# Layer 0 and layer 1 attention scores: distance bias added by VectorE instead of by flip products, with B's scores in two PSUM banks

## Chip, core and metric
The kernel runs on one core of a Trainium2 chip. Its time is the device time of one execution in microseconds (us), lower is better. The engines are TensorE (PE: matrix products and transposes; PEld is its weight load), VectorE (DVE), ScalarE (ACT), GpSimd (POOL) and SyncE (SP), whose queue issues nearly all DMAs. Each engine takes its own instructions in order, and semaphores join them.

## What is computed
A decoder trunk of two layers on 512 tokens of width 1024. Layer 0 has A (attention with a forget gate, 8 heads) and B (sliding window of 128, sinks, distance bias, 8 heads), layer 1 has C (sparse attention with a top-k mask and a distance bias, 8 heads) and D (latent attention, 8 heads). After each pair comes an output projection, then an MLP of width 4096. The change concerns the logits of B and C:

```python
# B: bias by distance, one sink logit per head in the softmax
bias = bias_table[_t5_bucket(jnp.maximum(dist, 0))]
logits = jnp.where(mask[None, :, None, None], logits + bias, -jnp.inf)
p = jax.nn.softmax(jnp.concatenate([logits, sink], axis=-1), axis=-1)[..., :-1]
# C: keys picked by top-k, bias by distance
bias = bias_table[_t5_bucket(jnp.maximum(dist, 0))].transpose(0, 1, 3, 2).astype(jnp.float32)
logits = jnp.where((dist >= 0)[:, :, None, :], logits + bias, -jnp.inf)
p = jax.nn.softmax(logits, axis=-1)
```

## The kernel before
Activations lie transposed in SBUF. Every fp32 operand is split into a rounded high part and a low remainder, and a product is three fp32r products (`product`, L677 to L679: high by high, low by high, high by low). A weight slab is 128 columns of a weight matrix: SP loads it (`load_slab`), ACT makes the high part (`split_slab`, L1161), POOL the low part (L1604), PE takes 8 tiles of it (24 products of 512 columns).

The heads are numbered j: A is 0 to 7, B 8 to 15, D 16 to 23, C 24 to 31. Both attention phases are software pipelines written out by hand, one step s per head. In step s of layer 0 (`first_step`), PE does scores(s+2), then the input slabs of that step (`SLABS_AT`: 18 in step 9, none in step 8 or from 10 on), then tiles of the output projection where `OUT_TILES_AT` places them as filling (steps 10 to 15), then values(s), then the transposes of the probabilities of head s+1 (`turn_probs`, L863). ACT does output_half(s-1), the high part of the transposed probabilities of s (`probs_hi`), the exponentials of s+2 (L1348) and output_hi(s-1). DVE does outputs_summed(s-1) (L2020), the low parts (`probs_lo`, L1795), then for B the reciprocal and the scaling of head s+1 (`normalise`, L1997 and L2004) and last the maxima of s+2 (L1986). In layer 1 (`heads`) the order is the same with fewer parts: DVE does probs_lo(s), maxima(s+2), outputs_summed(s-1), sums(s+2). The scaling goes through a diagonal that POOL makes, and PE's turning of the probabilities is L861.

Scores land in PSUM banks 0, 1 and 2 (`units(j)` says which query block stands where). scores(j) may write bank b once the exponentials of head j-1 have read it (L779, `exp_done`). The bias of a head comes from a row of 1024 words in DRAM (`bias_rows`), of which partition p reads a piece that starts at word p. That gives the strip in reversed query order. ACT makes its high part (`strip`, L1161), POOL its low part (`prepare`), and PE multiplies both with a reversed identity, `flip_r`, which turns the order round and adds the bias into the score bank: L789, L790, L792 to L795 for B, L816 and L817 for C. B's sink is a column beside each unit's scores, so its units are 130 or 258 columns wide.

Behind the heads of layer 0, slabs 19 and 20 are finished with the last tile of the attention output, slab 21 has its own spare place (`W_SPARE`), and slab 22 needs slot 0, which slab 20 holds. ACT splits slab 22 in `out_projection` only after the square and the rounding of output tile 0.

## Time and profile before
| | us |
|---|---|
| median of 3 runs (1240.57 to 1241.54) | 1240.57 |
| the profiled execution's own time | 1240.66 |
| its span, first to last instruction | 1238.9 |
| mean granted TensorE clock | 0.988 of full speed |

The profile is a page (busy time, chain, costliest groups) and a trace that answers questions. A timeline row has the start and the length of an instruction or of a run of equal ones (xN), its engine, line, operation, output<-inputs with sizes, and in square brackets how long its engine had been idle and who released it. Lengths of products overlap, since they are pipelined. What one costs a busy PE is the distance between two starts. PEclk is the share of the full 2.4 GHz granted in a window, and 0.5 is its other level, 1.2 GHz.

### The profile page before, as it was taken

Reading aid. Unit: us, or ns where it says so; the run is one execution under the profiler, and the core shown is the slowest. Engines: PE = TensorE matmul, PEld = TensorE weight load, DVE = VectorE, ACT = ScalarE, POOL = GpSimd, SP = SyncE. Lnnn points to the kernel's source line nnn. Section 1 sums busy time; section 2 is a strip of 40 time slices with the busy share of each in tenths; the row PEclk is TensorE's granted clock in tenths of the full one; section 3 lists DMA queues with packets and bytes.
Section 4 is the critical chain, followed back from the end, with each engine's and each line's share of the span. In section 5 each row is a group of like instructions: output and inputs, shape, how many; then the busy total and the mean of one; then the engine's idle time right before and its main releaser. Section 6 shows DMA issues by size and latency. Waiting matters only on the chain.

```text
span 1238.9 us, 16061 instructions
## 1 busy us (share of the span) xinstructions
PE 1193.5 (96%) x5744; PEld 983.7 (79%) x5749; DVE 674.3 (54%) x1023; ACT 515.3 (42%) x919; POOL 538.0 (43%) x291
## 2 busy tenths in 40 slices
PE   7999996999999999999998899999999999999997
PEld 5688885878888888888776678888788888888886
DVE  5766675665144154165669889556651441541654
ACT  6677575433222222224363467864332222222233
POOL 2333432334444444447632466434344444444441
PEclk9999998999999999999998999999999999999998
DMA  5222220333333333333312101102233333333332
GB/s 157 71 68 73 65 69 32 97 85 103 100 88 102 102 88 99 102 90 96 87 50 68 52 17 35 36 18 68 85 102 99 89 102 102 89 98 102 92 95 85
DMA packets 188922, 100.83 MB, mean 81 GB/s; under 512 B 8806, under 2 KB 186257, under 8 KB 188866
## 3 DMA queue, kind: packets, MB, share of 16 engines
q1 hardware_dynamic: 187596, 99.97, 28.0%
q8 instruction: 34, 0.56, 0.2%
q10 hardware_dynamic: 1270, 0.13, 0.1%
q14 instruction: 22, 0.18, 0.0%
HBM read 97.92 MB, written 2.16 MB: 81 GB/s over the span
## 4 chain that ended last, share of the span: by engine, by line
PE 74%; DVE 6%; ACT 3%; issue 1%; POOL 1%; DMA 0%; ACTq 0%; DVEq 0%; SPq 0%
PE bank L677 23%; PE bank L678 22%; PE bank L679 22%; PE bank L861 3%; DVE score L2101 1%; DVE best L2097 1%; ACT ur L1161 1%; ACT probs L1348 1%; POOL wl L1604 1%; DVE sqsum L1859 1%; PE bank L822 0%; ACT wh L1161 0%; PE bank L873 0%; PE bank L816 0%; PE bank L874 0%
## 5 line engine op out<-in xcount | busy, mean ns | idle before, releaser
L1604 POOL TENSOR_TENSOR wl<-raw,wh 128x1024 fp32r<-128x1024 f32 x172 | 419.7, 2441 | 554.1 <-ACT wh L1161 554.0
L677 PE MATMUL bank<-ur,wh 128*128 128x512 f32 x1080 | 422.2, 391 | 0.2 <-POOL wl L1604 0.2
L678 PE MATMUL bank<-ur,wh 128*128 128x512 f32 x1080 | 420.7, 390 | 0.0
L679 PE MATMUL bank<-ur,wl 128*128 128x512 f32 x1080 | 420.7, 390 | 0.0
L1161 ACT ACTIVATE wh<-raw 128x1024 fp32r<-128x1024 f32 x172 | 181.7, 1058 | 508.3 <-PE bank L679 508.1
L677 PEld LDWEIGHTS bank<-ur,wh 128*128 128x128 f32 x1080 | 203.2, 188 | 43.2 <-issue 1.1
L678 PEld LDWEIGHTS bank<-ur,wh 128*128 128x128 f32 x1080 | 203.2, 188 | 42.1 <-issue 0.5
L679 PEld LDWEIGHTS bank<-ur,wl 128*128 128x128 f32 x1080 | 203.0, 188 | 42.2
L1959 DVE TENSOR_TENSOR xT<-bank,xT 128x512 f32<-128x512 f32 x64 | 44.3, 692 | 227.6 <-PE bank L679 227.5
L1795 DVE TENSOR_TENSOR ur<-sq,ur 128x512 fp32r<-128x512 f32 x65 | 130.1, 2001 | 45.4 <-ACT ur L1161 45.4
L677 PE MATMUL bank<-xh,wh 128*128 128x512 f32 (+1 forms) x296 | 122.5, 414 | 5.3 <-DVE xl L1865 2.9
L678 PE MATMUL bank<-xl,wh 128*128 128x512 f32 (+1 forms) x296 | 117.3, 396 | 0.0
L679 PE MATMUL bank<-xh,wl 128*128 128x512 f32 (+1 forms) x296 | 117.3, 396 | 0.0
L1950 DVE TENSOR_TENSOR tbuf<-bank,rstd 128x512 f32<-128x512 f32 x64 | 44.2, 691 | 91.8 <-PE bank L679 91.4
L1348 ACT ACTIVATE probs<-bank,negmax 128x256 f32<-128x256 f32 (+5 forms) x128 | 63.5, 507 | 35.9 <-DVE negmax L1986 35.1
L677 PEld LDWEIGHTS bank<-xh,wh 128*128 128x128 f32 (+1 forms) x296 | 56.2, 190 | 23.0 <-issue 10.6
L1161 ACT ACTIVATE ur<-sq 128x512 fp32r<-128x512 f32 (+1 forms) x80 | 50.6, 632 | 39.2 <-DVE sq L1954 38.2
L679 PEld LDWEIGHTS bank<-xh,wl 128*128 128x128 f32 (+1 forms) x296 | 56.2, 190 | 13.1
L678 PEld LDWEIGHTS bank<-xl,wh 128*128 128x128 f32 (+1 forms) x296 | 56.3, 190 | 12.3 <-issue 1.3
L1795 DVE TENSOR_TENSOR probT_l<-bank,probT_h 128x512 fp32r<-128x512 f32 (+1 forms) x88 | 49.1, 600 | 27.6 <-ACT probT_h L1161 27.1
L1859 DVE TENSOR_TENSOR sqsum<-sqsum,sq 128x512 f32<-128x512 f32 x28 | 49.3, 1759 | 19.8 <-ACT sq L1200 19.8
L1986 DVE TENSOR_REDUCE negmax<-bank 128x1 f32<-128x256 f32 (+5 forms) x128 | 51.4, 458 | 6.0 <-PE bank L823 4.9
(226 smaller groups left out, 1365.4 us busy)
## 6 DMA issues: line engine op xcount, KB each, us to landing
raw<-in_w_mlp SPq DMA_DIRECT2D x128, 512.0 KB, 3.8
raw<-in_w_in_e SPq DMA_DIRECT2D x18, 512.0 KB, 3.6
raw<-in_w_in_o SPq DMA_DIRECT2D x10, 512.0 KB, 3.7
raw<-in_w_out_e SPq DMA_DIRECT2D x8, 512.0 KB, 3.7
raw<-in_w_out_o SPq DMA_DIRECT2D x8, 512.0 KB, 3.8
strip_raw<-bias_rows SPq DMA_DIRECT2D x8, 256.0 KB, 3.0
out<-probs SPq DMA_DIRECT2D x4, 512.0 KB, 2.6
probs<-in_x SPq DMA_DIRECT2D x2, 512.0 KB, 4.3
```

The lines of the kernel that those rows point to most:

```text
L677: mm(dst, lhs[0], rhs[0], start=start, stop=False, skip_group_check=not check)
L678: mm(dst, lhs[0], rhs[1], start=False, stop=False, skip_group_check=not check)
L679: return mm(dst, lhs[1], rhs[0], start=False, stop=stop, skip_group_check=not check)
L861: done = mm(dst, probs[:, slot, c:c + P], diag[slot][:, q:q + P], start=True, stop=True)
L1161: return nc.scalar.activation(dst, src, ACT.Copy, scale=scale)
L1348: e = nc.scalar.activation(probs[:, slot, pc:pc + w], bank[b][:, col:col + w], ACT.Exp, bias=negmax[:, slot, blk:blk + 1], accum_out=expsu ...
L1604: return nc.gpsimd.tensor_tensor(dst, a, b, ALU.subtract)
L1795: return v.tensor_tensor(dst, a, f(b), ALU.subtract)
L1859: v.tensor_tensor(sqsum[:, :], sqsum[:, :], sq[:, m % 2, :], ALU.add).then_inc(sq_added, 1)
L1950: v.tensor_tensor(t, ps, rstd[:, :], ALU.mult).then_inc(slab_taken, 1)
L1959: v.tensor_tensor(xT[:, m, :], ps, xT[:, m, :], ALU.add).then_inc(slab_taken, 1)
L1986: m = v.reduce_max(negmax[:, j % 2, blk:blk + 1], bank[b][:, col:col + w], AX.X, negate=True)
```

## The change
Seven edits belong together.

1. The rows of `bias_rows` are copied in DRAM 128 times each (`spread_bias`, 16 DMAs on SP's queue in steps -1 to 10), into `skew_b` and `skew_c`, whose pitch is one word longer than the copy. Reading with a pitch one shorter gives partition p a piece that starts p words earlier, in true order.
2. The flip products go, with `strip` on ACT, the strip part of `prepare` on POOL, and `strip_h` and `strip_l`.
3. DVE's maximum of a unit in B and C becomes one operation that computes -(score + bias), writes it back to the bank, and takes the minimum with a start value (the negated sink for B). The exponential then scales by -1.
4. The sink leaves the columns: ACT makes exp(sink - max) for 4 blocks (`sink_exp`), DVE adds it to the sums.
5. B's scores use banks 0 and 1 only, and slab 21's result goes to bank 2, so its tiles may run among the B heads.
6. The order of DVE in B changes: maxima(s+2) before probs_lo(s), and normalise(s+2) at the end of step s instead of normalise(s+1). Step 8 does both 9 and 10.
7. 14 tiles of the projection stand in steps 10 to 15 instead of 9, and the spare split of slab 21 moves from step 12 to step 10.

```diff
-SPARE_STEP = 12
-OUT_TILES_AT = {10: ((0, 0, 1),), 11: ((0, 1, 2),), 12: ((0, 2, 3),), 13: ((0, 3, 4),), 14: ((0, 4, 6),), 15: ((1, 0, 3),)}
-LAST_OUT_TILES = ((1, 3, 7), (0, 6, 7), (2, 0, 1))
+SPREAD_AT = {s: (2 * s + 2, 2 * s + 3) for s in range(-1, 3)}
+SPREAD_AT.update({s: (s + 5,) for s in range(3, 11)})
+SPARE_STEP = 10
+OUT_TILES_AT = {10: ((0, 0, 2),), 11: ((0, 2, 4),), 12: ((1, 0, 3),), 13: ((1, 3, 4), (2, 0, 1)), 14: ((2, 1, 4),),
+                15: ((0, 4, 6),)}
+LAST_OUT_TILES = ((1, 4, 7), (2, 4, 7), (0, 6, 7))
...
-                return [(0, 0, 0, 130, 0), (1, 0, 130, 258, 130), (2, 1, 0, 258, 388), (3, 2, 0, 258, 646)]
+                return [(0, 0, 0, 128, 0), (1, 0, 128, 256, 128), (2, 1, 0, 256, 384), (3, 1, 256, 256, 640)]
...
+            def spread_bias(i):
+                h = i % NH
+                rows, off, width = (skew_b, C_LEN, B_LEN) if i < NH else (skew_c, 0, C_LEN)
+                row = NH * (i // NH) + h
+                sp.dma_start(rows[h, :, 0:width], bias_rows[row:row + 1, off:off + width].to_broadcast([P, width]))\
+                    .then_inc(bias_spread, 16)
...
-                            mm(dst, flip_r[:, :], strip_h[:, slot, off:S], start=True, stop=False)
-                            mm(dst, flip_r[:, :], strip_l[:, slot, off:S], start=False, stop=False)
...
-            first_out_tiles(2, 1, KT)
+            first_out_tiles(2, KT - 1, KT)
...
+                    if attention(j) == "B" and i == 2:
+                        nc.scalar.activation(sink_exp[:, slot, :], negmax[:, slot, :], ACT.Exp,
+                                             bias=sink_in[:, j % NH:j % NH + 1])
...
-                    m = v.reduce_max(negmax[:, j % 2, blk:blk + 1], bank[b][:, col:col + w], AX.X, negate=True)
+                    if biased:
+                        width = 2 * W if attention(j) == "B" else S
+                        limit = sink_neg[:, j % NH:j % NH + 1] if attention(j) == "B" else -TAKEN
+                        m = v.tensor_tensor_reduce(logits, logits, strip_raw[:, slot, width - w:width], -1.0, limit,
+                                                   ALU.add, ALU.min, neg)
...
-                if NH <= s:
-                    if s + 1 < 2 * NH:
-                        normalise(s + 1)
-                    if s + 2 < 2 * NH:
-                        maxima(s + 2)
+                if s == NH:
+                    normalise(s + 1)
+                if NH <= s and s + 2 < 2 * NH:
+                    maxima(s + 2)
+                if 0 <= s:
+                    probs_lo(s, range(2))
+                if NH <= s and s + 2 < 2 * NH:
+                    normalise(s + 2)
```

What it moves stands below, before and now, for the places that the prediction speaks of. L numbers are those of each kernel's own file. First PE, the scores of one B head. Before, the bias products stand ahead of each block's own two:

```order
684 L792 MATMUL bank<-strip_h,flip_r 128x2
685 L793 MATMUL bank<-strip_l,flip_r 128x2
686 L794 MATMUL bank<-strip_h,flip_r 128x128
687 L795 MATMUL bank<-strip_l,flip_r 128x128
688 L799 MATMUL bank<-ur 128x128
689 L800 MATMUL bank<-ur 128x128
690 L789 MATMUL bank<-strip_h,flip_r 128x258
691 L790 MATMUL bank<-strip_l,flip_r 128x258
692 L799 MATMUL bank<-ur 128x256
693 L800 MATMUL bank<-ur 128x256
```
Now a whole head, behind the turning of the head before it, is:

```order
740 L868 MATMUL bank<-fixed,probs 128x128 x7
741 L807 MATMUL bank<-ur 128x128
742 L808 MATMUL bank<-ur 128x128
743 L807 MATMUL bank<-ur 128x256
744 L808 MATMUL bank<-ur 128x256
```
The ten bias products of a head are gone, and 8 of 18 products are left (of which 4 are shown).

Next DVE in a B step, from the sum of a head's output on. Before:

```order
145 L2020 TENSOR_TENSOR sq<-bank,sq 64x512
146 L1795 TENSOR_TENSOR probT_l<-bank,probT_h 128x512
147 L1795 TENSOR_TENSOR probT_l<-bank,probT_h 128x384
148 L1997 RECIPROCAL rsum<-expsum 128x4
149 L2004 TENSOR_SCALAR probs<-probs,rsum 128x130
150 L2004 TENSOR_SCALAR probs<-probs,rsum 128x258 x3
151 L1986 TENSOR_REDUCE negmax<-bank 128x1 x4
```
Now (the last two of the four units' maxima stand first, each with its accumulator read, the instruction that has only `negmax`):

```order
208 L1975 ISA bank,negmax<-bank,strip_raw,sink_neg 128x256
209 L1975 ISA negmax 128x1
210 L1975 ISA bank,negmax<-bank,strip_raw,sink_neg 128x256
211 L1975 ISA negmax 128x1
212 L1775 TENSOR_TENSOR probT_l<-bank,probT_h 128x512
213 L1775 TENSOR_TENSOR probT_l<-bank,probT_h 128x384
214 L1990 TENSOR_TENSOR sink_exp<-sink_exp,expsum 128x4
215 L1991 RECIPROCAL rsum<-sink_exp 128x4
216 L1998 TENSOR_SCALAR probs<-probs,rsum 128x128
217 L1998 TENSOR_SCALAR probs<-probs,rsum 128x256 x3
```
The maxima moved ahead of the low parts, and the scaling that follows belongs to a head one later.

Last DVE in a C step. Before:

```order
517 L1795 TENSOR_TENSOR probT_l<-bank,probT_h 128x512 x2
518 L1795 TENSOR_TENSOR probT_l<-bank,probT_h 128x256
519 L1986 TENSOR_REDUCE negmax<-bank 128x1 x4
520 L2020 TENSOR_TENSOR rope<-bank,rope 64x512
521 L1997 RECIPROCAL rsum<-expsum 128x4
```
Now, in one of the first C steps, which has no output sum:

```order
574 L1775 TENSOR_TENSOR probT_l<-bank,probT_h 128x512 x2
575 L1775 TENSOR_TENSOR probT_l<-bank,probT_h 128x256
576 L1975 ISA bank,negmax<-bank,strip_raw 128x128
577 L1975 ISA negmax 128x1
578 L1975 ISA bank,negmax<-bank,strip_raw 128x384
579 L1975 ISA negmax 128x1
580 L1975 ISA bank,negmax<-bank,strip_raw 128x256
581 L1975 ISA negmax 128x1
582 L1975 ISA bank,negmax<-bank,strip_raw 128x512
583 L1975 ISA negmax 128x1
584 L1991 RECIPROCAL rsum<-expsum 128x4
```
The order of DVE in C is as it was, with eight instructions for four.

## Rows read from the trace of the kernel before

**Rows 1.** The page's part 1: busy us, share of the span, instructions.
```profile
PE 1193.5 (96%) x5744; PEld 983.7 (79%) x5749; DVE 674.3 (54%) x1023; ACT 515.3 (42%) x919; POOL 538.0 (43%) x291
```

**Rows 2.** Waits of PE from 160 to 217 us: total us, times, longest us.
```profile
PE bank L873 <- DVE probT_l L1795: 5.4, 4, 2.7
...
PE bank L863 <- DVE probs L2004: 3.6, 6, 1.4
...
PE bank L792 <- ACT probs L1348: 2.6, 4, 0.7
```

**Rows 3.** Timeline of PE in a B head's scores: start us, length us.
```profile
153.39 0.28 PE L799 MATMUL bank<-ur 128*128 128x256 f32 x1
...
153.63 0.28 PE L789 MATMUL bank<-strip_h,flip_r 128*128 128x258 f32 x1
```

**Rows 4.** Timeline of ACT and DVE over one step of the B heads.
```profile
188.57 0.37 ACT L1348 ACTIVATE probs<-bank,negmax 128x130 f32<-128x130 f32 x1 [2.36 <-DVE negmax L1986]
...
190.28 0.63 ACT L1161 ACTIVATE ur<-sq 64x512 fp32r<-64x512 f32 x1
...
191.55 0.69 DVE L2020 TENSOR_TENSOR sq<-bank,sq 64x512 f32<-64x512 f32 x1 [2.42 <-ACT sq L1161]
...
192.28 1.16 DVE L1795 TENSOR_TENSOR probT_l<-bank,probT_h 128x512 fp32r<-128x512 f32 x2
...
193.56 1.08 DVE L2004 TENSOR_SCALAR probs<-probs,rsum 128x130 f32<-128x130 f32 x4
...
194.55 1.29 DVE L1986 TENSOR_REDUCE negmax<-bank 128x1 f32<-128x130 f32 x4
```

**Rows 5.** Windows: length; busy PE, PEld, DVE, ACT, POOL; PEclk; DMA; GB/s.
```profile
46.00:49.00 3.00, 1.96 (x9) 1.67 (x10) 1.62 (x3) 0.99 (x2) 2.51 (x2) 0.85 0.00 0
...
212.00:216.00 4.00, 4.00 (x14) 3.25 (x13) 1.16 (x2) 1.72 (x3) 0.00 (x0) 0.58 0.54 157
```

**Rows 6.** Timeline of PE, DVE and ACT over one step of the C heads.
```profile
797.70 1.62 DVE L1795 TENSOR_TENSOR probT_l<-bank,probT_h 128x512 fp32r<-128x512 f32 x3 [1.63 <-ACT probT_h L1161]
...
799.25 1.09 DVE L1986 TENSOR_REDUCE negmax<-bank 128x1 f32<-128x128 f32 x3
...
799.59 0.39 PE L816 MATMUL bank<-strip_h,flip_r 128*128 128x512 f32 x1
...
800.10 0.58 PE L822 MATMUL bank<-ur,xh 128*128 128x512 f32 x1
...
800.10 0.37 ACT L1348 ACTIVATE probs<-bank,negmax 128x128 f32<-128x128 f32 x1 [1.16 <-DVE negmax L1986]
...
802.48 0.63 ACT L1161 ACTIVATE xh<-rope 64x512 fp32r<-64x512 f32 x1
...
804.23 1.62 DVE L1795 TENSOR_TENSOR probT_l<-bank,probT_h 128x512 fp32r<-128x512 f32 x3 [1.57 <-ACT probT_h L1161]
```

**Rows 7.** Groups of DVE by shape: busy us, mean ns of one.
```profile
L1986 DVE TENSOR_REDUCE negmax<-bank 128x1 f32<-128x512 f32 x24 | 16.5, 685 | 4.5 <-PE bank L823 4.2 <-PE bank L812 0.2
...
L1795 DVE TENSOR_TENSOR probT_l<-bank,probT_h 128x512 fp32r<-128x512 f32 x56 | 36.7, 686 | 19.5 <-ACT probT_h L1161 19.0
...
L2101 DVE MATCH_VALUE_LOAD score<-best,score 128x8 f32 x48 | 4.1, 84 | 0.6
...
L1938 DVE TENSOR_TENSOR_SCAN rstd_q<-sq,probs 64x512 f32<-64x512 f32 x1 | 1.2, 1216 | 0.0
```

**Rows 8.** Timeline: marks of steps 7 to 15 and of the projection.
```profile
160.30 0.39 PE L873 MATMUL bank<-probT_h,ur 128*128 128x512 f32 x1
...
169.82 0.40 PE L677 MATMUL bank<-xh,wh 128*128 128x512 f32 x1
...
216.77 0.45 PE L677 MATMUL bank<-ur,wh 128*128 128x512 f32 x1
...
221.81 0.69 DVE L1975 TENSOR_TENSOR xT<-bank,xT 128x512 f32<-128x512 f32 x1 [2.13 <-PE bank L679]
...
227.41 0.47 PE L677 MATMUL bank<-ur,wh 128*128 128x512 f32 x1 [0.20 <-POOL wl L1604]
```

More of the change, by code:

```diff
@@ L412, in pj @@
                 return bank[1 + n - N_OUT1]
+            if n == N_OUT0 + 2:
+                return bank[2]
             return bank[4 + n % 4]
@@ L427, in attention, with score_banks, banks_before @@
             return "ABDC"[j // NH]
+        def score_banks(j):
+            return 2 if attention(j) == "B" else 3
+        def banks_before(j):
+            return sum(score_banks(i) for i in range(j))
         def pt_parts(j):
@@ L510, in strip_count @@
             return sum(1 for i in range(j + 1) if attention(i) in "BC" and i % 2 == j % 2)
-        def t5_rank(j):
-            return sum(1 for i in range(j) if attention(i) in "BC")
-        def prep_rank(j):
-            return sum(1 for i in range(j) if attention(i) in "ABC")
         def out_bank(j):
@@ L639, in _ @@
                     load_slab(n + 3)
-                if NH <= s + 5 < 2 * NH:
-                    if s + 5 == NH:
-                        sp.wait_ge(bias_stored, 16)
+                if s == -1:
+                    sp.wait_ge(bias_stored, 16)
+                for i in SPREAD_AT.get(s, ()):
+                    spread_bias(i)
+                if NH <= s + 4 < 2 * NH:
+                    if s + 4 == NH:
+                        sp.wait_ge(bias_spread, 16 * NH)
                         sp.wait_ge(fg_in, 3)
-                    load_strip(s + 5)
+                    load_strip(s + 4)
             load_slab(N_OUT0 + 3)
@@ L1425, in heads @@
                         probs_hi(s)
-                    if first <= s + 3 < last and attention(s + 3) == "C":
-                        strip(s + 3)
                     if latent(first, s + 3):
@@ L1738, in _ @@
             for s in FIRST_STEPS:
[L1739 removed]
+                if s + 3 < NH:
                     prepare(s + 3)
@@ L1996, in sums @@
                     dve.wait_ge(probs_ready, 4 * (j - 1))
-                v.reciprocal(rsum[:, j % 2, :], expsum[:, j % 2, :]).then_inc(rsum_ready, 1)
+                if attention(j) == "B":
+                    own.link(v.tensor_tensor(sink_exp[:, j % 2, :], sink_exp[:, j % 2, :], expsum[:, j % 2, :], ALU.add))
+                v.reciprocal(rsum[:, j % 2, :], (sink_exp if attention(j) == "B" else expsum)[:, j % 2, :]).then_inc(rsum_ready, 1)
             def normalise(j):
```

131 lines of the change are left out of this document (51 added, 80 removed).

## The prediction
> **What bounds the kernel now.** I read the page's busy shares first, then the waits of PE, then timelines of the two attention phases, the clock last. PE is busy for 1193.5 of 1238.9 us [rows 1], and almost everywhere it simply runs through its products. There work taken from PE is time. The exception is the end of layer 0's attention: from 160 to 217 us PE waits 11.6 us in all (5.4 for the low parts, 3.6 for the scaling, 2.6 for the exponentials) [rows 2]. There DVE and ACT set the pace, each in the other's way: one B step goes exponentials (ACT, from 188.57), output (190.28), output sum (DVE, 191.55), low parts (192.28), scaling (193.56), maxima (194.55), and then the next exponentials [rows 4]. The two bracketed idle times in rows 4 are each engine waiting for the other.
>
> The C phase looks bound by PE, which has no wait in it. But the reader should add up the loop of the other two [rows 6]: low parts begin at 797.70, maxima at 799.25 (1.55 later), the first exponential at 800.10 (0.85), the rounding of the output at 802.48 (2.38), and the next head's low parts at 804.23 (1.75, in which ACT does that rounding, 0.63, the half output, and the first high part). That makes 6.53 us. In it I see only one pause that PE causes, about 0.1 us before the last exponential. So in C PE and the DVE-ACT loop take nearly the same time per head, and freeing PE alone gives about 0.1.
>
> **The change part by part.** The sum is made against the profiled execution's own 1240.66 us, 1.8 more than its span and 0.1 above the median.
>
> *Bias products.* Two products lie between 153.39 and 153.63 [rows 3], 0.12 us each. Ten go per B head: 1.2 us, 9.6 for eight. In C the pair of 512 columns takes 0.51 (799.59 to 800.10) [rows 6]; a head has 1280 columns of pairs, 2.5 times as many, so 1.3 us, 10.2 for eight. Where it counts differs:
>
> a) Heads 8 and 9 have their scores in steps 6 and 7, behind which input slabs keep PE busy: **-2.4**.
>
> b) Step 8 has no slab and no filling tiles, and DVE now does scaling 9, maxima 10, low parts 8 in a row. Before, from the end of values(7) (1.3 us after 160.30, so 161.6) to slab 18 (169.82) it took 8.2 us [rows 8]. Now: half output and sum 1.5, reciprocal and scaling 2.3 (an estimate: 0.2, gaps, and the scaling at 1.08 in rows 4, lengthened by POOL's work), maxima 1.6, first low part 0.7, values 1.1, turning 0.8, scores 1.0. That is 9.0: **+0.8**.
>
> c) In that chain PE stands idle for about 4.5 us between scores(10) and values(8). Two rows show what follows such pauses: in 46 to 49 us PE was busy for 1.96 of 3 us and the mean granted clock fell to 0.85, and in 212 to 216, behind the waits of rows 2, it was 0.58 [rows 5], that is mostly at 1.2 GHz. The second row costs 0.42 of 4 us, 1.7. I take one and a half such stretches behind step 8: **+2.4** (bounds 0 and 3.4).
>
> d) Steps 9 to 15. Before, 169.82 to 216.77 [rows 8], 47.0 us, with most of the 11.6 us of waits and with one stretch at the low clock. Now DVE's step is: sum 0.72, maxima, low parts 1.15, two small operations 0.4, scaling 1.1 to 1.3. The maxima were 1.24 (start of 194.55 plus 1.29, less the overlap) [rows 4]. A pass over 512 elements costs 685 ns as a maximum and 686 as a two-input operation with PSUM [rows 7], so the new operation's main part costs nothing more. The accumulator read is not in this trace. Its nearest row is the tiny MATCH_VALUE_LOAD at 84 ns, and the upper bound is 0.17 us, the length of a reciprocal of four columns if it has to drain. I take 0.08, four per head, 1.56 in all. A step is then 5.0 us, since ACT's exponentials now run while DVE does the low parts. PE's own step of 1.0 scores, 1.4 to 2.0 tiles, 0.95 values, 0.8 turning is shorter than that. Step 9: slab, values, turning, 7.2. Then 4.9; 7.0 (the spare split, 1.06, and the last query's copies, 1.3, now meet in step 10 and delay the next); 5.0; 5.1; and 3.8 and 2.6 for the last two, which have no scores. Sum 35.6: **-11.3**.
>
> e) The projection behind it. Five tiles of 0.68 moved ahead, which leaves PE only two tiles after slab 19 is done. Slab 22 needs a chain from there: 221.81 (slab 19's addition) to 227.41 (slab 22's first product), 5.6 us [rows 8]; before, it was covered but for 0.2. Now 7 + 1 tiles (5.5) and that chain (5.7) make 11.2 to 11.4 from the end of values(15), against 10.6 (216.77 to 227.41): **+0.8**. PE idles 4.2 us there, and pays one stretch at the low clock: **+1.7** (bounds 0 and 3.4).
>
> f) C. Three steps before 791 took 7.0 us, with PE ahead of the loop; they can fall to the loop's 6.5, -1.5. The loop grows by the accumulator reads of the first bank, two per head, 0.16 (bounds 0.1 and 0.34), and loses the 0.1 pause: eight heads, +0.5 to +1. **-0.5** (bounds -2 and +2). The strips that ACT and POOL no longer split lay in idle time: ACT waited 1.16 us for the maxima behind it [rows 6]. Nothing.
>
> g) The copies in DRAM: 16 DMAs, 4.2 MB, on SP's queue between slab loads, over some 120 us in which windows show a DMA share of 0 to 0.5 [rows 5]. Slabs are loaded three ahead. Nothing, up to +2 if a slab comes late. Strip loads now wait for maxima(j-2), behind them the loads of slabs 20 to 22 queue, each more than a step early: nothing.
>
> Sum: -2.4 + 0.8 + 2.4 - 11.3 + 0.8 + 1.7 - 0.5 = **-8.5**, 1232.2 against 1240.66, **1232** against the median.
>
> The Trainium skill, TensorE: Matmul & The Clock Gate, in its part on how the oscillation bites, says that short bursts of products between waits bring PE back to half rate again and again. The rows above bear it out twice. By that rule the change, which makes PE's bursts shorter and its waits longer in steps 8 to 13, would pay the clock more often than my sum has it, and it is the third rival.
>
> **Rivals.**
> 1. *PE sets the pace everywhere.* All bias products come out as time, waits stay as they are: 1240.6 - 9.6 - 10.2 = 1221. For it: no wait of PE in C. Against: the sum of rows 6.
> 2. *The new operation is slow.* The one scan in the trace, whose result also feeds back from element to element, takes 1216 ns for 512 elements against 686 [rows 7], so about one more cycle per element. On 896 elements of a B head that is 0.93 us for six heads on the loop (5.6), on C's 1280 about 0.95 of 1.33 on the loop (7.6). 1232 + 13 = 1245, **slower** than before. It decides from 0.6 us more per head (8.5 us over 14 heads). Against: the scan has to carry a product and a sum, a minimum only one value, and plain maxima and two-input operations are equal.
> 3. *The clock.* Two or three more stretches at 1.2 GHz, in steps 11 to 13, at 1.7 each: 1236. For it: a wait of 2.9 us that I expect in step 11.
> 4. *The copies delay a slab*: 1234.
> 5. *DVE's new order doesn't help*: ACT's high parts come late, and the B step stays near 6.7 less only what PE saved. Then d) is about -4 instead of -11.3: 1239, no change.
>
> [...]
>
> **How the numbers follow.** Forecast 0.46 (its own range 1227 to 1237); rival 1 0.15; rival 2 0.11; rival 3 0.15; rival 4 0.05; rival 5 0.08. Predicted is the likeliest, 1232. The range 1221 to 1241 leaves out rival 2 and the faster half of rival 1, some 2 in 10. About 0.2%, 2.5 us, is what a measurement of this kernel can tell from no change, so faster is below 1238.1 and slower above 1243.1. Faster: 0.46 + 0.15 + 0.11 + 0.04 + 0.03 and a little over, 0.80; same 0.09; slower 0.11.
>
> **What would show it.** In the profile after: the strip groups and flip products gone; a new DVE group of some 690 ns at 512 columns and a read near 80 ns (rival 2: over 1 us). B steps 10 to 13 near 5 us, values(8) after a wait over 3 us, a wait of some 4 us for slab 22's low part. The granted clock below 1 behind both. In C the distance of low parts 6.5 to 6.7 us, with PE waits of 1.2 us per head that before had none. If the C distance falls to 5.5, my loop is wrong, and with it 8 us of the sum.

## Result, and the profile after
The changed kernel takes 1237.23 us (median of 7 runs, 1236.33 to 1238.81), the kernel before 1240.57: a ratio of 0.9972, interval 0.9962 to 0.9983. It is faster by 3.3 us where 8.5 were forecast. The time lies inside the range of 1221 to 1241, and the direction is right, but most of the expected gain is missing. The profiled execution's span is 1235.2 us, against 1238.9.

First the page of the changed kernel, part 1, then its waits of PE from 160 to 228 us (total us, times, longest). They answer to [rows 1] and [rows 2]:

```profile
PE 1177.4 (95%) x5601; PEld 967.1 (78%) x5605; DVE 680.6 (55%) x1094; ACT 508.0 (41%) x910; POOL 522.1 (42%) x267
```

```profile
PE bank L878 <- DVE probT_l L1775: 12.2, 4, 4.9
PE bank L695 <- POOL wl L1599: 4.2, 1, 4.2
```

PE has 16.1 us less to do, and the time fell by less than a quarter of that. Waits for the scaling and the exponentials are gone, but those for the low parts have more than doubled, from 5.4 to 12.2 us. Their places stand in PE's timeline, with the marks that answer to [rows 8] (start, length, [idle before <- who released]):

```profile
166.53 0.36 PE L878 MATMUL bank<-probT_h,ur 128*128 128x256 f32 x1 [4.34 <-DVE probT_l L1775]
...
170.81 0.39 PE L695 MATMUL bank<-xh,wh 128*128 128x512 f32 x1
...
190.48 0.36 PE L878 MATMUL bank<-probT_h,ur 128*128 128x256 f32 x1 [4.86 <-DVE probT_l L1775]
...
203.28 0.36 PE L878 MATMUL bank<-probT_h,ur 128*128 128x256 f32 x1 [2.01 <-DVE probT_l L1775]
...
224.26 0.47 PE L695 MATMUL bank<-ur,wh 128*128 128x512 f32 x1 [4.21 <-POOL wl L1599]
```

These are step 8 (then slab 18), step 11, step 13, and slab 22. Behind each, the windows (columns as in [rows 5]) show the low clock:

```profile
164.00:168.00 4.00, 1.47 (x9) 1.50 (x10) 3.58 (x15) 2.63 (x10) 0.14 (x1) 0.86 0.24 57
188.00:192.00 4.00, 1.52 (x9) 1.55 (x10) 3.58 (x16) 2.52 (x10) 0.53 (x1) 0.85 0.25 64
192.00:196.00 4.00, 4.00 (x22) 3.78 (x22) 2.66 (x11) 2.04 (x6) 0.00 (x0) 0.72 0.34 100
204.00:208.00 4.00, 4.00 (x17) 3.49 (x17) 3.17 (x9) 2.69 (x5) 0.96 (x1) 0.57 0.00 0
224.00:228.00 4.00, 3.74 (x10) 2.99 (x11) 4.00 (x3) 0.00 (x0) 2.89 (x2) 0.62 0.44 131
```

The new operation is as fast as hoped. DVE's groups by shape, beside [rows 7] (busy us, mean ns of one):

```profile
L1975 DVE DVE_READ_ACCUMULATOR2_ANT negmax<- 128x1 f32 x64 | 9.0, 141 | 0.0
L1975 DVE CUSTOM_DVE_ANT_0 bank<-bank,strip_raw 128x512 f32<-128x512 f32 x8 | 5.9, 733 | 0.0
```

It takes 733 ns at 512 columns, 48 more than the plain maximum, and not the 1216 of the scan. So the missing gain isn't there. It is in DVE's timeline at the end of step 10 (with POOL's rows of the same stretch):

```profile
182.83 1.07 DVE L1998 TENSOR_SCALAR probs<-probs,rsum 128x128 f32<-128x128 f32 x4
...
183.94 3.46 DVE L1775 TENSOR_TENSOR ur<-tbuf,ur 64x512 fp32r<-64x512 f32 x2
...
184.21 2.64 POOL L1599 TENSOR_TENSOR ur<-raw,ur 128x1024 fp32r<-128x1024 f32 x1 [4.14 <-ACT ur L1166]
...
186.81 1.71 POOL L1599 TENSOR_TENSOR ur<-sq,ur 128x512 fp32r<-128x512 f32 x1
187.43 0.69 DVE L2014 TENSOR_TENSOR sq<-bank,sq 64x512 f32<-64x512 f32 x1
```

The two subtractions for the last query block take 3.46 us. In the kernel before the same two took 1.39:

```profile
182.32 1.39 DVE L1795 TENSOR_TENSOR ur<-tbuf,ur 64x512 fp32r<-64x512 f32 x2
```

What is new is POOL beside them: its spare split, which the change moved here from step 12, runs from 184.21 to 186.85. Output sum, maxima and low parts of head 11 all stand behind them on DVE, and PE waits 4.86 us for those.

### The profile page after: what moved, and what is told of

It is laid out like the page before. It is cut to its first block, busy times and chain, and to the rows that moved or that the text cites. A ratio compares the mean times of both kernels' runs of the same rounds, so it can differ in the third digit from the quotient of the medians.

```text
span 1235.2 us, 15811 instructions
## 1 busy us (share of the span) xinstructions
PE 1177.4 (95%) x5601; PEld 967.1 (78%) x5605; DVE 680.6 (55%) x1094; ACT 508.0 (41%) x910; POOL 522.1 (42%) x267
## 4 chain that ended last, share of the span: by engine, by line
PE 82%; DVE 9%; ACT 5%; issue 2%; POOL 1%; DMA 1%; SPq 0%; ACTq 0%; DVEq 0%
PE bank L695 25%; PE bank L697 25%; PE bank L696 25%; ACT probs L1347 2%; PE bank L866 1%; PE bank L868 1%; ACT ur L1166 1%; DVE probT_l L1775 1%; PE bank L878 1%; DVE score L2096 1%; PE bank L879 1%; DVE bank L1975 1%; DVE best L2092 1%; POOL wl L1599 1%; DMA tbuf<-in_x 1%
## 5 line engine op out<-in xcount | busy, mean ns | idle before, releaser
L697 PEld LDWEIGHTS bank<-ur,wl 128*128 128x128 f32 x1080 | 203.2, 188 | 42.2
L1347 ACT ACTIVATE probs<-bank,negmax 128x256 f32<-128x256 f32 (+3 forms) x128 | 63.3, 506 | 39.6 <-DVE negmax L1975 27.8
L695 PEld LDWEIGHTS bank<-xh,wh 128*128 128x128 f32 (+1 forms) x296 | 56.8, 192 | 24.9 <-issue 10.6
L1166 ACT ACTIVATE ur<-tbuf 64x512 fp32r<-64x512 f32 (+2 forms) x68 | 42.3, 627 | 20.1 <-DVE tbuf L2077 11.2
```

Of the source, the lines that this page charges most:

```text
L695: mm(dst, lhs[0], rhs[0], start=start, stop=False, skip_group_check=not check)
L697: return mm(dst, lhs[1], rhs[0], start=False, stop=stop, skip_group_check=not check)
L1166: return nc.scalar.activation(dst, src, ACT.Copy, scale=scale)
L1347: e = nc.scalar.activation(probs[:, slot, pc:pc + w], bank[b][:, col:col + w], ACT.Exp, bias=negmax[:, slot, blk:blk + 1], scale=sign, acc ...
```

## The ledger
Between marks of both traces, in us. Steps 9 to 15 run from slab 18's first product to the end of values(15). The last column is the kernel of experiment 11, in which POOL no longer stretches DVE in steps 9 to 15, and nothing else is changed.

| | before | forecast | after | no stretching |
|---|---|---|---|---|
| start to the end of values(7) | 161.7 | -2.4 | 160.5 (-1.2) | |
| step 8, to slab 18 | 8.1 | 11.4 | 10.3 | 10.9 |
| step 9 | 7.1 | 7.2 | 7.1 | 7.1 |
| step 10 | 5.9 | 4.9 | 5.2 | 5.2 |
| step 11 | 6.8 | 7.0 | 10.3 | 8.4 |
| step 12 | 6.7 | 5.0 | 5.4 | 6.1 |
| step 13 | 7.9 | 5.1 | 6.7 | 4.9 |
| step 14 | 8.1 | 3.8 | 4.9 | 3.8 |
| step 15 | 4.5 | 2.6 | 2.7 | 2.7 |
| steps 9 to 15 | 47.0 | 35.6 | 42.2 | 38.1 |
| values(15) to slab 22 | 10.6 | 11.4 | 11.3 | 11.3 |
| slab 22 to the MLP's first sums | 31.7 | 33.4 | 33.3 | |
| scores(24) to the out projection | 58.8 | -0.5 | 56.5 (-2.3) | |

Between the MLP's first sums and scores(24) both kernels take 511.2 us (both with the spell of low clock near 670 us, and each with one of its own, before near 720 us and after near 608), and behind layer 1's heads 409.8 and 409.9. Steps 9 to 15 are short of the forecast by 6.6 us. Every other line is within 1.8 of it.

## Experiments
Each begins with what was expected, as written before it ran. Profiles are read between marks, since the whole time also moves by chance (last experiment). Ratios are to the kernel before. The changed kernel's own is 0.9972, and 0.9977 (0.9967 to 0.9988) when run again beside the last group. Most intervals are 0.1 to 0.2% either side, so single edits of 1 to 3 us are judged by the marks.

**1. POOL's spare split one step later**
```diff
-SPARE_STEP = 10
+SPARE_STEP = 11
```


> The changed kernel, with the spare split of slab 21 moved from step 10 to step 11, and nothing else. It asks why step 11 took 10.25 us where 7.0 were forecast. Theory one (two engines that stretch each other): in step 10 the two subtractions of DVE for the last query block took 3.46 us instead of 1.39 while POOL made the spare slab's low part (2.64 us, start 184.21); what is late by that is late on the chain to values(11). Then here the two subtractions take about 1.4 us, PE's wait before values(11) falls from 4.86 to 2 to 3 us, the low clock behind it shortens, scores(15) starts 2 to 3.5 us earlier than at 198.72, and the whole is 1.5 to 3.5 us shorter (ratio to the kernel before 0.9945 to 0.996), if the split does not meet another operation of DVE in its new place. Theory two (step 11 is long by the order of the work alone, the last query's copies and the output sum): 3.46 stays or its loss comes back elsewhere, and the whole is within 0.6 us of the changed kernel's 1237.2.

Ratio 0.9972 (0.996 to 0.9985), span 1232.6. DVE and POOL at the end of step 10:

```profile
182.62 2.12 DVE L1998 TENSOR_SCALAR probs<-probs,rsum 128x128 f32<-128x128 f32 x4
...
182.90 1.41 POOL L1599 TENSOR_TENSOR ur<-sq,ur 128x512 fp32r<-128x512 f32 x1 [3.06 <-ACT ur L1166]
...
184.76 1.38 DVE L1775 TENSOR_TENSOR ur<-tbuf,ur 64x512 fp32r<-64x512 f32 x2
```

The subtractions are back at 1.38, and step 11 is 8.6 us instead of 10.3. But PE's wait before values(11) is still 3.81, where I expected 2 to 3. POOL's other pass, the pair's low part, now falls on the scaling, which takes 2.12 instead of 1.07 (in experiment 11, without that, the wait is 2.79). From the end of values(7) to slab 22 it takes 60.6 us, 3.2 less than in the changed kernel (63.8). The span is shorter by 2.6, the measured time by nothing that the interval shows, so the forecast of 1.5 to 3.5 us for the whole isn't borne out. Theory one holds for the place alone.

**2. POOL's pair pass behind the scaling**, on top of 1
```diff
                 if 2 <= s and s % 2 == 0:
+                    if NH <= s < 2 * NH - 2:
+                        pool.wait_ge(probs_ready, 4 * (s + 3))
                     output_lo(s - 1)
```


> The kernel with the spare split in step 11, in which POOL also makes the low parts of a pair's output (128x512, 1.41 us) only when DVE has scaled the head after the next: steps 8, 10 and 12. DVE's scaling (four operations, 1.07 us alone) took 2.09 to 2.12 us in just those steps. Theory (POOL and DVE stretch each other when DVE's operation has all its operands in SBUF, and not when one is in PSUM): the scaling takes 1.07 in steps 8, 10 and 12, the output sum, maxima and low parts beside the moved work keep 0.69, 1.6 and 1.15, slab 22 starts 1.5 to 3 us before 220.85, and the whole is 1 to 3 us shorter than with the spare split alone. Rival (what stretches DVE is ACT's copies, or the data are late): scaling stays near 2.1, nothing gained; or the low parts now stretch from 1.15 to 1.7 or more.

Ratio 0.9963 (0.9949 to 0.9978), span 1235.2:

```profile
183.49 1.07 DVE L2000 TENSOR_SCALAR probs<-probs,rsum 128x128 f32<-128x128 f32 x4
...
184.59 2.38 DVE L1777 TENSOR_TENSOR ur<-tbuf,ur 64x512 fp32r<-64x512 f32 x2
184.64 1.79 POOL L1599 TENSOR_TENSOR ur<-sq,ur 128x512 fp32r<-128x512 f32 x1 [3.92 <-DVE probs L2000]
```

The scaling is at 1.07 in all three steps, as the theory says. The subtractions that follow it in steps 8 and 10 took its place, at 2.36 and 2.38. In step 12, where none follow, PE's wait before values(13) fell from 1.71 to 0.90. From values(7) to slab 22: 60.9, no gain. The collision had only moved on, which my expectation had missed. The subtractions too have all their operands in SBUF, so by its own theory they had to be stretched.

**3. The query's subtractions in step 11**, on top of 1
```diff
                     probs_lo(s, range(2))
+                if s == NH + 3:
+                    projected(placed(18) - 1, EVEN[18][0], 18)
...
-                    if n not in V_INSIDE:
+                    if n not in V_INSIDE and n != 18:
```


> The kernel with the spare split in step 11, in which DVE makes the last query block's low parts (two subtractions, 1.38 us) in step 11 between the low parts of head 11 and the scaling of head 13, where it waits for exponentials anyway, instead of at the end of step 10. It asks how much of step 11 (8.56 us there, 7.0 forecast) stands behind them. Theory: PE's wait of 3.81 us before values(11) falls to 2.4 or 2.6, step 11 becomes 7.2, and step 12 grows by at most 0.7; slab 22 starts 0.7 to 1.5 us earlier. Rival: what stands before values(11) is ACT's chain (query copies 1.3, output, high parts), and the wait stays; or step 12 grows by the whole 1.4.

Ratio 0.9977 (0.9966 to 0.9988), span 1236.4. PE's wait before values(11) fell to 2.42, and step 11 from 8.6 to 6.8. But scaling 13 now fell on the whole spare split and took 3.24 us (1.07 alone, POOL's pass 2.40), PE waited 3.55 before values(12), and step 12 grew from 5.8 to 9.4. In all 61.8 from values(7) to slab 22, 1.2 more than without the edit. The forecast for step 12 was wrong by the same cause: what is stretched is set by who happens to meet POOL.

**4. Low parts first in step 8**
```diff
                 if s == NH:
+                    probs_lo(s, range(2))
                     normalise(s + 1)
                 if NH <= s and s + 2 < 2 * NH:
                     maxima(s + 2)
-                if 0 <= s:
+                if 0 <= s and s != NH:
                     probs_lo(s, range(2))
```


> The changed kernel, in which DVE makes the low parts of head 8 first in step 8, and the scaling of head 9, the maxima of head 10 and its scaling after them. It asks whether step 8 (10.4 us from values(7) to slab 18, 8.2 before) is long by DVE's order alone. Theory: the low parts no longer stand behind the scaling and four maxima (2.1 and 1.6 us), PE's wait of 4.34 us before values(8) falls to about 1 us, slab 18 starts 2 to 4 us earlier, and what is left behind it depends on the exponentials of head 10, which now start as before. Whole: 1.5 to 3 us shorter than the changed kernel. Rival: the turning of head 9 and the exponentials of head 10 take the place of the wait, because the chain scaling, maxima, exponentials is what sets steps 9 and 10: slab 18 earlier, but scores(13) within 0.5 us of 183.07, and the whole within 0.6 us.

Ratio 0.9976 (0.9962 to 0.9991), span 1233.4. PE's timeline in step 8:

```profile
161.06 0.36 PE L878 MATMUL bank<-probT_h,ur 128*128 128x256 f32 x1 [0.53 <-DVE probT_l L1775]
...
162.83 0.98 PE L868 MATMUL bank<-fixed,probs 128*128 128x128 f32 x7 [0.64 <-DVE probs L1998]
...
164.66 0.30 PE L807 MATMUL bank<-ur 128*128 128x128 f32 x1 [0.85 <-ACT probs L1347]
...
166.62 0.63 PE L695 MATMUL bank<-xh,wh 128*128 128x512 f32 x1
```

One wait of 4.34 became four short ones of 2.3 in all, and step 8 took 7.8 us instead of 10.3. Not all of it is the order. In the changed kernel DVE's tiny addition of the sinks to the sums stood in step 8 beside POOL's pass for a weight slab, and took 0.98 us (DVE, then POOL, both in the changed kernel):

```profile
161.88 0.98 DVE L1990 TENSOR_TENSOR sink_exp<-sink_exp,expsum 128x4 f32<-128x4 f32 x1
```

```profile
160.46 2.37 POOL L1599 TENSOR_TENSOR wl<-raw,wh 128x1024 fp32r<-128x1024 f32 x1 [5.88 <-ACT wh L1166]
```

It ends 0.03 us behind POOL's pass. With the low parts ahead of it, it comes when the pass is over and takes 0.15, so up to 0.8 us of the gain are POOL's. And the rival came in part: step 9 took 8.3 us instead of 7.1 with the low clock now on slab 18's products (0.72 and 0.85 from 164 to 172 us), and by the end of step 12 only 0.6 of the 2.5 us were left. Steps 13 and 14 are 1.9 us shorter, where the changed kernel has a spell of low clock (0.57) and this one has none. From values(7) to slab 22 it takes 61.3. The measured time doesn't show it (its runs spread from 1233.2 to 1240.1).

**5. The projection's tiles and slab 22**
```diff
-LAST_OUT_TILES = ((1, 4, 7), (2, 4, 7), (0, 6, 7))
+LAST_OUT_TILES = ((1, 4, 7), (0, 6, 7))
...
-            first_out_tiles(2, KT - 1, KT)
+            first_out_tiles(2, 4, KT)
...
-                    elif m == 1:
+                    elif m == (0 if n0 == N_OUT0 else 1):
```


> The changed kernel with two edits behind the heads of layer 0: output tiles 4 to 7 of slab 21 are multiplied behind slab 20 again, as in the kernel before, so that seven tiles stand between slab 19's last and slab 22, and ACT splits slab 22 as soon as slot 0 is free, before the square and the rounding of output tile 0. It prices term e of the prediction. Theory: the wait for slab 22's low part falls from 4.2 to under 1.5 us, and the spell of low clock behind it (window 224 to 228, PEclk 0.62) goes: slab 22 starts 2.5 to 4 us earlier, and the whole is 3.5 to 5.5 us shorter than the changed kernel, some 1232.5. Rival: the clock does not come back with the wait, or ACT's earlier split delays tile 0's rounding so that another wait follows: 1.5 to 2.5 us shorter, or nothing.

Ratio 0.9955 (0.9943 to 0.9967), span 1232.9:

```profile
221.45 0.47 PE L695 MATMUL bank<-ur,wh 128*128 128x512 f32 x1 [1.06 <-POOL wl L1599]
...
224.00:228.00 4.00, 4.00 (x19) 3.31 (x18) 3.24 (x6) 1.98 (x3) 0.11 (x1) 1.00 0.56 160
```

The wait is 1.06 and the clock behind it is full. Slab 22 starts 2.8 us earlier (from values(7) to there it takes 60.7) and the MLP's first sums 4.4. Term e stood on the right chain. The whole is only 2.3 us shorter by the span, where I expected 3.5 to 5.5: behind the first sums 2.1 us came back, in code that the edits don't touch.

**6. PE kept busy in its waits**
```diff
+                fill = {NH: 16, NH + 3: 18}.get(s, 0)
+                if fill:
+                    pe.wait_ge(exp_done, banks_before(NH))
+                for _ in range(fill):
+                    mm(bank[2][:, :], xh[:, 0, 0:P], xh[:, 0, :], start=True, stop=True)
                 if 0 <= s:
                     first_values(s)
```


> The changed kernel with products added that nothing reads: 16 in step 8 and 18 in step 11, each 128 columns by 512, into the idle bank 2, just ahead of PE's waits for the low parts (4.34 and 4.86 us, in which PE stood idle). It prices the low clock alone (term c, and its share of d). Theory: products of 0.22 us fill 3.5 and 3.9 us of the waits, the waits themselves end at the same time, and behind them PEclk is 1.00 instead of 0.65 to 0.80; values, turning and scores after them are 1.6 us shorter in step 8 and 1.8 in step 11, of which DVE's and ACT's own chain keeps half. Slab 22 starts 1.5 to 3.5 us earlier than at 224.26. Rival: the values and turning behind the waits are not on the path that decides (DVE is), and it moves by less than 0.7.

Ratio 0.9956 (0.994 to 0.9972), span 1236.0. PE in step 8, then the windows of step 8 and step 11:

```profile
160.08 3.81 PE L1010 MATMUL bank<-xh 128*128 128x512 f32 x16
164.60 0.36 PE L878 MATMUL bank<-probT_h,ur 128*128 128x256 f32 x1 [0.71 <-DVE probT_l L1780]
...
167.29 0.40 PE L695 MATMUL bank<-xh,wh 128*128 128x512 f32 x1
```

```profile
164.00:168.00 4.00, 3.40 (x27) 3.30 (x28) 3.58 (x9) 3.28 (x11) 1.40 (x1) 1.00 0.73 217
...
188.00:192.00 4.00, 4.00 (x28) 3.43 (x26) 3.84 (x16) 2.79 (x9) 0.00 (x0) 1.00 0.50 152
```

From values(8) to slab 18 it takes 2.69 us instead of 4.28, and from values(11) to values(12) 5.30 instead of 6.56. So the low clock alone cost 1.6 us in step 8 and 1.3 in step 11. Slab 22 came 4.5 us earlier, of which 1.95 stood there already at the end of values(7) by chance. In its own stretch it is 2.6 of these 2.9, so the DVE-ACT loop kept almost none of it, against my "half".

**7. Freeing PE alone, in B.** The kernel before without B's bias products:
```diff
-                        if c0 == 0:
-                            mm(dst, flip_r[:, :], strip_h[:, slot, 0:258], start=True, stop=False)
-                            mm(dst, flip_r[:, :], strip_l[:, slot, 0:258], start=False, stop=False)
...
-                        mm(dst[:, 2:width], qh, kb[0][:, kv, ks], start=False, stop=False)
-                        last = mm(dst[:, 2:width], qh, kb[1][:, kv, ks], start=False, stop=True)
+                        mm(dst, qh, kb[0][:, kv, 0:width], start=True, stop=False)
+                        last = mm(dst, qh, kb[1][:, kv, 0:width], start=False, stop=True)
```


> The kernel before, in which PE leaves out the bias products of the B heads; strips are still loaded and split and all orders stay. B's logits lack bias, and the sink columns hold products of no meaning. It measures how much of the gain between values(7) and slab 22 (65.7 us before, 63.8 in the changed kernel) comes from freeing PE alone, without the new order and the two banks. Theory: PE's scores stand in the loop exponentials, scores, maxima, exponentials, so the 1.2 us per head count nearly whole in steps 8 to 13: this stretch is 4 to 7 us shorter than in the kernel before, as much as or more than the changed kernel gained, and the new order gave nothing in net. Rival: as forecast, the old order of DVE holds the step near 6.5 us whatever PE does, and the stretch is at most 2.5 us shorter; then the new order is what gained.

Ratio 0.9999 (0.9988 to 1.001), span 1240.2. Its waits of PE from 160 to 217 us, beside [rows 2]:

```profile
PE bank L861 <- DVE probT_l L1783: 6.3, 6, 2.0
PE bank L851 <- DVE probs L1992: 4.4, 5, 1.2
PE bank L787 <- ACT probs L1336: 1.3, 2, 0.7
```

My theory fell, and the forecast's reading stood: the stretch from values(7) to slab 22 took 65.0 us instead of 65.7. Of the 9.6 us of products 1.0 was gained in step 8, and steps 9 to 15 took 47.3, no less than before (47.0). The rest came back as waits and as low clock (PEclk 0.50 to 0.95 in nine windows of 4 us from 176 to 216). What the changed kernel gained in steps 9 to 15 needed more than a freed PE. It came with the new order, the two banks and the moved tiles together; no run takes these apart.

**8. Freeing PE alone, in C.** The kernel before without C's bias products:
```diff
-                            mm(dst, flip_r[:, :], strip_h[:, slot, off:S], start=True, stop=False)
-                            mm(dst, flip_r[:, :], strip_l[:, slot, off:S], start=False, stop=False)
```


> The kernel before, with the bias products of the C heads left out on PE alone, so that C's logits lack the distance bias; the strips are still loaded and split, and DVE's maxima stay plain ones. It measures what freeing PE is worth in C. My loop theory (low parts, maxima, exponentials, rounding of the output set C's pace; 1.3 us of PE per head are hidden): the distance of low parts in the middle of C stays at 6.4 to 6.55 us, PE now waits about 1.2 us per head there, and the whole is 1.5 to 3.5 us shorter than before, from C's first heads alone. Rival (PE sets the pace): the distance falls to some 5.2 to 5.5 us, PE still has no waits, and the whole is 8 to 10 us shorter.

Ratio 0.999 (0.9981 to 0.9998), span 1237.5. DVE's low parts in this kernel, two heads running, then in the changed one:

```profile
794.68 1.62 DVE L1793 TENSOR_TENSOR probT_l<-bank,probT_h 128x512 fp32r<-128x512 f32 x3 [1.56 <-ACT probT_h L1159]
800.98 1.62 DVE L1793 TENSOR_TENSOR probT_l<-bank,probT_h 128x512 fp32r<-128x512 f32 x3 [1.57 <-ACT probT_h L1159]
```

```profile
787.86 1.62 DVE L1775 TENSOR_TENSOR probT_l<-bank,probT_h 128x512 fp32r<-128x512 f32 x3 [1.57 <-ACT probT_h L1166]
794.27 1.62 DVE L1775 TENSOR_TENSOR probT_l<-bank,probT_h 128x512 fp32r<-128x512 f32 x3 [1.56 <-ACT probT_h L1166]
```

The distance is 6.30 with no bias at all and 6.42 in the changed kernel. Before it is 6.53 [rows 6] and 6.67 in turn, for the head behind those of rows 6 begins here:

```profile
810.90 1.62 DVE L1795 TENSOR_TENSOR probT_l<-bank,probT_h 128x512 fp32r<-128x512 f32 x3 [1.63 <-ACT probT_h L1161]
```

The loop sets the pace; the new operations and their reads together cost it 0.12 per head. PE, freed of 1.3 us per head, waits instead (0.65 to 0.9 us for POOL's diagonal here, 0.80 and 1.02 for the low parts in the changed kernel). The whole gained 1.1 us, a little less than my lower end.

**9. The three edits together** (1, 4 and 5)

> The three edits together: spare split in step 11, the tail's tiles and ACT's earlier split, and low parts first in step 8. In the traces each moved the first low parts of layer 1 by -3.4 (718.78), -3.6 (718.51) and -4.1 us (718.03) against the changed kernel's 722.15. If they are independent (they lie in steps 11, behind 15, and 8) that mark stands at 711 to 712, and the whole, with 1.2 us given back to the clock in layer 1 as in each of the three, is 8 to 11 us shorter than the changed kernel: 1226 to 1229, ratio to the kernel before 0.989 to 0.991. Rival: they remove the same wait twice (a wait and the low clock behind it, of which only one can be had), and the sum is 5 us or less: 1232.

Ratio 0.9917 (0.9899 to 0.9935), span 1230.9. From values(7) to slab 22: 58.7 us, against 60.6, 61.3 and 60.7 for each alone. The separate gains of 3.2, 2.5 and 3.1 make 8.8, and 5.1 came. The whole is 6.8 to 7.4 us shorter than the changed kernel by the ratios, where 8 to 11 stood. So it lies between theory and rival. In steps 8, 10 and 12 the scaling takes 2.11 or 2.12, and PE waits 1.70, 3.78 and 1.99 us for the low parts in steps 10, 11 and 13.

**10. POOL's pair pass behind the output sum**, on top of 9
```diff
                 if 2 <= s and s % 2 == 0:
+                    if NH <= s < 2 * NH - 2:
+                        pool.wait_ge(o_sum, s + 1)
                     output_lo(s - 1)
```


> The three edits of the combined kernel, and POOL makes the low parts of a pair's output in steps 8, 10 and 12 only when DVE has summed the output of the same step, so that it runs beside maxima and low parts, whose operands are partly in PSUM. Waiting for the scaling alone had only moved the collision on to the query's subtractions (2.36 and 2.38 us instead of 1.38). Theory: no operation of DVE from 160 to 215 us is stretched any more (scaling 1.07 to 1.08, subtractions 1.38 to 1.39 in every step), maxima and low parts keep 1.6 and 1.15, steps 10 and 12 are 1 us shorter each, from the end of values(7) to slab 22 it takes 55.5 to 57.5 us (58.7 in the combined kernel), and the whole is 1 to 3 us shorter than that kernel, which stands at 0.9917 of the kernel before. Rival: DVE's operations with one operand in PSUM stretch too beside POOL (none has stood beside a POOL pass in the B steps so far except the output sum), and nothing is gained.

Ratio 0.989 (0.9872 to 0.9907), span 1226.9:

```profile
181.68 1.07 DVE L2000 TENSOR_SCALAR probs<-probs,rsum 128x128 f32<-128x128 f32 x4
182.78 1.39 DVE L1777 TENSOR_TENSOR ur<-tbuf,ur 64x512 fp32r<-64x512 f32 x2
...
184.97 1.27 POOL L1599 TENSOR_TENSOR ur<-sq,ur 128x512 fp32r<-128x512 f32 x1 [6.06 <-DVE sq L2016]
185.20 0.49 DVE L1977 CUSTOM_DVE_ANT_0 bank<-bank,strip_raw,sink_neg 128x256 f32<-128x256 f32 x1
```

No scaling or subtraction is stretched in any step, and neither are the maxima beside POOL's pass, 0.49 as elsewhere, which read and write a bank. POOL's pass itself is at 1.27 to 1.30 instead of 1.39 to 1.79. From values(7) to slab 22: 54.7 us.

**11. Stretching alone**: the changed kernel with only the edits of experiments 1 and 10

> The changed kernel with POOL's passes moved and nothing else: the spare split in step 11, and the pair's low parts in steps 8, 10 and 12 behind DVE's output sum. It takes out the stretching of DVE alone, to give its share of the 6.5 us by which steps 9 to 15 missed the forecast. From the end of values(7) to slab 22 the changed kernel takes 63.8 us, 60.6 with the spare split moved; the combined kernel fell from 58.7 to 54.7 by the other passes. Theory: nothing of DVE is stretched from 162 to 215 us; steps 9 to 15 (slab 18's start to the end of values(15)) fall from 42.2 to 37.5 to 39 us, values(7) to slab 22 to 57.5 to 59.5, and the whole is 2.5 to 5 us shorter than the changed kernel, chance spells aside. Rival (the combined kernel's 4.0 us came from its other edits, which here are missing): steps 9 to 15 stay above 40.

Ratio 0.9955 (0.9942 to 0.9969), span 1233.3. Steps 9 to 15 take 38.1 us (table above), as the theory has it: 4.1 less, 3.2 of them from the spare split. From values(7) to slab 22 it is 60.2, 0.7 above my bound, since step 8 grew to 10.9 behind a low clock:

```profile
164.00:168.00 4.00, 3.32 (x16) 3.35 (x17) 3.57 (x10) 2.97 (x10) 0.00 (x0) 0.50 0.72 221
188.00:192.00 4.00, 4.00 (x21) 4.00 (x20) 2.27 (x9) 2.82 (x5) 2.37 (x1) 0.50 0.46 136
```

The second row is what is left of steps 11 and 12. Values and turning there take 3.10 us where experiment 6 with its full clock takes 1.67, and scores and tiles behind them 1.2 us more. By this estimate step 11 would be 7.0 at full clock and step 12 4.8; forecast were 7.0 and 5.0. In step 8 the addition of the sinks is still at 0.98. The whole is 2.1 to 2.7 us shorter than the changed kernel by the ratios, where 2.5 to 5 stood.

**12. The best version**: 10, with nine idle products ahead of step 11's wait, as in 6

> The kernel with POOL behind the output sum, and nine products of 128x512 into the idle bank 2, which nothing reads, ahead of PE's wait in step 11 (3.78 us in the combined kernel, some 2.8 expected here). Theory: PEclk stays 1.00 behind that wait, and values(11), turning and scores take 1.2 us less; 0.5 to 1.2 us shorter than without the nine products. Rival: the remaining wait is short enough that no spell follows it even without them, and nothing changes, or the spell comes behind the wait in step 13 instead.

Ratio 0.9895 (0.9877 to 0.9912), the same as 10 within the interval. The wait in step 11 fell from 2.78 to 0.69 and the stretch from values(7) to slab 22 to 53.3 us, and its profile, 1220.6, is the shortest of all, but its runs reach from 1222.5 to 1229.6. Of the 1.4 us by which the stretch is shorter, 0.8 stood there ahead of the nine products: kernel 10 had a spell of low clock on slab 18 (0.64) and this profile has none. Steps 11 and 12 gave 0.5. So the nine products show nothing in the time. Kernel 10, at 1226.8, beats both kernels of this case.

**13. The changed kernel again**

> The changed kernel once more, unaltered, to see how much its profile varies by itself, since in the runs so far stretches of low clock stood at places where the code had not been changed (near 12, 20, 48, 608 and 816 us), and cost 1.2 to 1.7 us each. Theory one: the spells behind the waits of steps 8, 11 and 13 and behind slab 22's come again within 0.1 in PEclk, those elsewhere come and go, and the span is 1233 to 1237. Theory two: each kernel has its fixed pattern, and span, marks and spells are those of the first profile within 0.5 us.

1237.55 us (1235.51 to 1240.55), span 1237.7. Marks up to the last C scores are within 0.3 us of the first profile. Window 816 to 820 of the first profile, then of the second:

```profile
816.00:820.00 4.00, 2.67 (x23) 2.47 (x22) 2.77 (x11) 3.01 (x10) 2.70 (x3) 1.00 0.44 131
```

```profile
816.00:820.00 4.00, 2.67 (x15) 2.37 (x14) 3.06 (x12) 2.72 (x10) 2.69 (x4) 0.84 0.44 131
```

The same code at the same time, with the same busy time of PE, got another clock. The second profile is 1.3 us later at the last low parts of layer 1, and 2.5 at the end. So neither theory holds alone: up to 616 us the pattern of low windows came again within 0.02 (that near 20 us too, which ten of the other thirteen kernels lack), and from 668 us on the spells differ.

## Why the prediction was off
**Step d failed, by its size.** Forecast -11.3, measured -4.8. The mechanism (maxima ahead of low parts, exponentials beside them) was right as far as the runs show: freeing PE alone gave nothing in these steps (47.3 us in experiment 7), and with the stretching taken out steps 10, 13, 14 and 15 take 5.2, 4.9, 3.8 and 2.7 us, for 4.9, 5.1, 3.8 and 2.6. The forecast durations, taken from rows where POOL stood still, did not hold. "Scaling 1.1 to 1.3" was 2.1 in step 12, and the 1.4 us of subtractions in step 10 were 3.46. Experiment 11 puts this at 4.1 of the 6.6 us. The other 2.5 are the low clock behind the wait in step 11, by the estimate there; no run has a full clock and no other edit. The nearest is the kernel of experiment 12, with low parts first in step 8, idle products in step 11, nothing stretched and the full clock all the way: its steps 8 to 15 take 44.9 us, and the forecast without its clock term is 9.0 + 35.6 = 44.6. I had expected that wait (2.9 us; it was 4.86, and 2.79 without the stretching), but priced what follows it only as a rival: "two or three more stretches at 1.2 GHz". Rival 3's time, 1236, is the one nearest to the result, for less than half of its cause.

The warning stood in the trace of before, in step 12, where the same two passes of POOL lay then (DVE, then POOL):

```profile
201.35 2.05 DVE L2004 TENSOR_SCALAR probs<-probs,rsum 128x130 f32<-128x130 f32 x4
```

```profile
198.92 2.37 POOL L1604 TENSOR_TENSOR ur<-raw,ur 128x1024 fp32r<-128x1024 f32 x1 [5.26 <-ACT ur L1161]
201.24 1.28 POOL L1604 TENSOR_TENSOR ur<-sq,ur 128x512 fp32r<-128x512 f32 x1
```

The scaling also took 1.57 (179.53) and 1.85 (209.01) beside POOL, and 1.08 in three steps where at most the last 0.2 us of a pass lay beside it. From such rows one reads a price per meeting, not a range. The Trainium skill, SBUF — State Buffer, in its section on who interferes with whom, has the rule that was missing from my sum: an instruction of DVE with two SBUF inputs, or one in a mode that takes both ports, and a GpSimd instruction that reads SBUF shut each other out for the whole instruction. By it the second subtraction of step 10 would begin when POOL's split ends, at 186.85, and with 0.69 us of its own end at 187.5. The trace agrees: they ended at 187.40. The page also exempts an instruction with at most one SBUF input outside those modes, and the maxima of experiment 10 agree.

**a)** Forecast -2.4, measured -1.2. PE no longer covers the last part of A's low parts and waits 0.42 and 0.48 us for it in steps 6 and 7.

**b) and c)** Forecast +3.2, measured +2.2. With the clock kept up, step 8 took 8.8 us (experiment 6), where 9.0 stood in the sum. The clock cost 1.6, not 2.4. Here the sum did allow for POOL: 2.3 for reciprocal and scaling, and 2.3 it was. But the scaling took its 1.07, and what POOL lengthened was the addition ahead of it (0.98), so that term was right by luck. In d) the sum made no such allowance.

**e)** Right: a wait of 4.21 against 4.2, +0.6 against +0.8 for the chain, and 1.6 against 1.7 for the clock. Experiment 5 gave it back.

**f)** Forecast -0.5, measured -2.3. The first three steps fell from 7.0 to 6.4 as forecast. The loop didn't grow by 0.16 per head but shrank from 6.53 and 6.67 in turn to 6.42. The 6.53 of rows 6 was the shorter of the two, and one head was read as all. The 0.1 us pause before the last exponential, behind PE's long scores, is gone, as the sum had it. The accumulator read of 141 ns (80 in the sum) overlaps the next operation, so that a head costs 0.12 more than with no bias. Rivals 1 (products are time) and 2 (slow operation) are out by experiment 8 and the 733 ns.

**g)** No slab and no strip was late. Right.

**Rival 5** had nearly the right number (-4 for d) and the wrong reason. The Trainium skill, TensorE: Matmul & The Clock Gate, in the part on how the oscillation bites, had spoken for paying the clock more often. Here it was paid behind three waits in steps 8 to 13, where the sum had one; by that rule rival 3 would have been the forecast.

## What to carry to other kernels
A duration read from a trace belongs to what the other engines did beside it: before a pass of POOL is moved, list the operations of DVE that it will meet, and price those with all operands in SBUF at their own time plus nearly all of POOL's undisturbed time. The shortest operation counts too: 0.16 us became 0.98. A gain on the busiest engine counts only as far as the loop of the other two lets it through. A wait that a forecast leaves on TensorE, as long as those that the trace shows with low clock behind them, has to carry that clock in the sum and not as a rival.

## What the runs showed of the chip
- DVE's operations with all operands in SBUF grow, beside a pass of POOL, by 0.8 to 0.9 of the time that this pass takes undisturbed (1.28 or 2.37 us). Four scalings: 1.07 us alone, 2.12 beside a pass of 1.41, 3.24 beside 2.40. Two subtractions: 1.38 alone, 2.38 beside 1.79, 3.46 beside 2.64. An addition of four columns: 0.16 alone, 0.98 in a pass that had 0.95 us to go. Output sum (0.69), low parts (1.15) and the new maxima (0.49), each with an operand in a bank, keep their time. POOL's pair pass itself goes from 1.28 to between 1.39 and 1.79.
- The accumulator read is recorded with 141 ns but starts together with the next operation; against a loop without any bias a C head pays 0.12 us for the four new operations and their reads.
- The low clock behind the same pause comes in one execution and not in another. The windows near 608 us are full in the kernel before and in two others; in the other twelve the lowest is at 0.50 to 0.79, in code that no edit touches. Such a spell cost 1.0 us near 816, 1.3 and 1.6 in experiment 6 and 1.6 behind slab 22, as much as the edits one wants to measure.
- Products that nothing reads held the granted clock at 1.00 through pauses of 4.3 and 4.9 us, and of the 1.6 and 1.3 us that this saved 2.6 reached slab 22.
